# One encoder trunk on one core: the loading stage and the first input stage put into one program per engine

## The reference

```python
hn = rms_norm(x, norm_mix[0])                      # y = x * rsqrt(mean(x*x) + 1e-6) * gain
proj = hn @ w_in                                   # 2560 columns: u (1024), q, k, v (512 each)
u = u[..., :512] * sigmoid(u[..., 512:])           # the gating ("glu")
u = silu(layer_norm(depthwise_conv(u, width=31) + conv_b, ln_g, ln_b))
lam = exp(sum(lq1 * lk1)) - exp(sum(lq2 * lk2)) + 0.2
a = softmax(q0 k0 + bias) - lam * softmax(q1 k1 + bias)   # 4 heads, T5 bias from a 32-bucket table
h = h + concat(u, rms_norm(a @ v)) @ w_out         # then cross-attention on 256 tokens `mem`, then MLP
# layer 1: RWKV-7, forward and backward scans over 512 tokens, 16 heads of 64
w_pre = w0 + tanh(xw @ w1) @ w2                    # low-rank ("lora") pair for the decay
a_pre = a0 + (xa @ a1) @ a2                        # and for the in-context learning rate
```

## Time and profile before

| | |
|---|---|
| median of 3 runs | 2039.53 us |
| profiled execution, its own time | 2042.42 us |
| its span | 2040.6 us |
| PE busy | 1913.6 us (94%) |
| DVE busy | 1033.9 us (51%) |
| ACT busy | 740.0 us (36%) |
| POOL busy | 174.9 us (9%) |
| mean granted TensorE clock | 0.973 of full |

### The profile page before, as it was taken

How to read it: one execution, slowest core, us unless ns; L and a number is a source line. 1 busy time by engine, 2 the same in 40 slices (tenths; PEclk the granted TensorE clock), 3 DMA queues, 4 the chain that set the end, 5 groups by cost and what they waited for, 6 DMA issues and landing times. The chain is left out here.

```text
span 2040.6 us, 38376 instructions
## 1 busy us (share of the span) xinstructions
PE 1913.6 (94%) x16921; PEld 1544.4 (76%) x16921; DVE 1033.9 (51%) x1382; ACT 740.0 (36%) x991; POOL 174.9 (9%) x136
## 2 busy tenths in 40 slices
PE   6899799999999999899979999999689999999998
PEld 4788557778888888657758888889558778888886
DVE  4794365434433432464528877787254344424422
ACT  4331475325321332133733333332263334213322
POOL 1000002001000001220002311111001010000000
PEclk8999899999999999999989999999899999999998
DMA  5223414203332332244231111110443122332321
GB/s 181 83 83 124 144 55 158 92 22 102 103 104 87 99 104 85 101 147 149 78 129 42 47 47 47 48 47 25 144 175 104 42 83 83 103 103 83 104 83 41
DMA packets 162974, 187.82 MB, mean 92 GB/s; under 512 B 9657, under 2 KB 150118, under 8 KB 161402
## 3 DMA queue, kind: packets, MB, share of 16 engines
q1 hardware_dynamic: 159008, 172.48, 25.9%
q0 software_dynamic: 3152, 12.71, 1.6%
q10 hardware_dynamic: 650, 0.19, 0.0%
HBM read 160.18 MB, written 20.99 MB: 89 GB/s over the span
## 5 line engine op out<-in xcount | busy, mean ns | idle before, releaser
L332 DVE TENSOR_TENSOR weights_lo<-w,weights_hi 128x2048 fp32r<-128x2048 f32 x108 | 247.3, 2290 | 225.3 <-ACT weights_hi L319 225.3
L319 ACT ACTIVATE weights_hi<-w 128x2048 fp32r<-128x2048 f32 x110 | 210.2, 1911 | 259.9 <-PE ps L347 250.0
L345 PE MATMUL ps<-x_hn_hi,weights_hi 128*128 128x512 f32 x640 | 252.8, 395 | 0.0
L347 PE MATMUL ps<-x_hn_hi,weights_lo 128*128 128x512 f32 x640 | 249.2, 389 | 0.0
L346 PE MATMUL ps<-x_hn_lo,weights_hi 128*128 128x512 f32 x640 | 249.1, 389 | 0.0
L346 PE MATMUL ps<-f_hidden_lo,weights_hi 128*128 128x512 f32 x512 | 199.2, 389 | 0.0
L345 PE MATMUL ps<-f_hidden_hi,weights_hi 128*128 128x512 f32 x512 | 199.2, 389 | 0.0
L347 PE MATMUL ps<-f_hidden_hi,weights_lo 128*128 128x512 f32 x512 | 199.2, 389 | 0.0
L1461 DVE SCALAR_TENSOR_TENSOR f_relu<-ps,x_squares 128x512 f32<-128x512 f32 x64 | 44.1, 691 | 191.2 <-PE ps L347 172.6
L345 PEld LDWEIGHTS ps<-x_hn_hi,weights_hi 128*128 128x128 f32 x640 | 120.2, 188 | 26.3 <-issue 1.4
L346 PEld LDWEIGHTS ps<-x_hn_lo,weights_hi 128*128 128x128 f32 x640 | 120.2, 188 | 26.1 <-issue 1.4
(11 more groups left out here) (328 smaller groups left out, 3477.6 us busy)
## 6 DMA issues: line engine op xcount, KB each, us to landing
w<-in_ffn_w_up_dram SPq DMA_DIRECT2D x32, 1024.0 KB, 5.5
w<-in_ffn_w_down_dram SPq DMA_DIRECT2D x32, 1024.0 KB, 5.1
w<-in_xattn_w_kv_dram SPq DMA_DIRECT2D x16, 1024.0 KB, 5.4
w<-in_ab_w_in_dram SPq DMA_DIRECT2D x10, 1024.0 KB, 5.0
w<-in_xattn_w_q_dram SPq DMA_DIRECT2D x8, 1024.0 KB, 5.0
w<-in_xattn_w_o_dram SPq DMA_DIRECT2D x8, 1024.0 KB, 5.0
w<-in_ab_w_out_dram SPq DMA_DIRECT2D x4, 1024.0 KB, 5.4
w<-in_rwkv_w_r_dram SPq DMA_DIRECT2D x4, 1024.0 KB, 6.8
```

Source lines behind the costliest of these rows:

```text
L319: act.activation(hi, raw, ACT.Copy).then_inc(k.w_hi_ready, 1)
L332: eng.tensor_tensor(lo, raw, hi.bitcast(F32), ALU.subtract).then_inc(k.w_lo_ready, 1)
L345: pe.matmul(out, lhs[0], rhs[0], start=start, stop=False)
L347: return pe.matmul(out, lhs[1], rhs[0], start=False, stop=stop)
```

## The change

Four things are done in one diff.

1. The two blocks become one. The norm's root comes from sums over the rows of `x`: ACT squares the untransposed rows with an accumulating sum (L680), takes Ln and Exp of the 128x4 result, DVE scales four identity matrices by it (`x_roots`), and PE multiplies ones by these, which leaves the root of every token on all partitions in PSUM bank 7; the norm reads it there. PE transposes the parameter rows first, then `x`. DVE takes five of the eight transposed chunks out of the banks, ACT three. The bias table rows ("b") and lambda's sums ("l") move into `seq` behind i2. The small loads move from ACT's queue to SP's, and SP loads one weight slot ahead of them and two behind.
2. `glu(1)` stands after 24 steps of the convolution.
3. POOL no longer waits for the memory values at the stage's end. ACT (before the first write over the region) and POOL (at its own end) wait for them in the next stage. SP issues the bias reload ahead of the last three weight slots.
4. In the scan the lora tiles of pair p + 2 are issued behind the later of W and A of pair p.

```diff
 class Norm:                       # start_dve
-        dve.wait_ge(self.s_rs, 1)
...
-                                         self.rs[:, 1, :], ALU.mult, ALU.mult).then_inc(self.s_t, 1)
+                                         k.ps[:, 7, :], ALU.mult, ALU.mult).then_inc(self.s_t, 1)
 def stage_in(k, cat):
         for n in range(16):
             seq.append(("i", n))
+            if n == 2:
+                seq += [("b", 0), ("b", 1), ("l", 0)]
...
             def _(sp):
-                sp.dma_start(k.con[:, :], i["consts"]).then_inc(s_con, 16)
+                sp.dma_start(k.con[:, 0:3 * P], i["consts"][:, 0:3 * P]).then_inc(s_con, 16)
...
+                sp.wait_ge(s_root, 1)
+                k.wait_full(sp, jx + C - 1)
+                sp.dma_start(mn, i["mem"][0].rearrange("(a p) d -> p a d", p=P)).then_inc(s_m, 16)
+                k.load_weights(sp, k.at)
+
+                sp.wait_ge(s_tvo, 16)
+                sp.wait_ge(s_ktout, 16)
+                sp.dma_start(k.bias[:, :, :], ...).then_inc(k.s_bias, 16)
+                k.load_weights(sp, k.at + NW)
...
             def _(pe):
+                pe.wait_ge(s_diag, 4)
+                for a in range(4):
+                    m = pe.matmul(k.ps[:, 7, a * P:(a + 1) * P], k.ones, diag[:, a, :], start=True, stop=True)
+                m.then_inc(s_rs, 1)
                 mm3_first(pe, k, j0, ws, hn, lambda c: nrm.wait(pe, c))
...
             def _(act):
+                act.wait_ge(s_eps, 1)
+                warm_ln(k, act)
+                for a in range(4):
+                    act.wait_ge(s_x[a], 16)
+                    k.act.link(act, act.activation(xsq[:, :], xn[:, a, :], ACT.Square, accum_out=xst[:, a:a + 1]))
+                k.act.link(act, act.activation(xst[:, 4:8], xst[:, 0:4], ACT.Ln, bias=k.eps[:, 0:1], scale=1.0 / D))
+                act.activation(xst[:, 8:12], xst[:, 4:8], ACT.Exp, scale=-0.5).then_inc(s_root, 1)
+                for c in (4, 6, 7):
+                    k.wait_full(act, jx + c)
+                    act.activation(k.h[:, c, :], k.bank(jx + c), ACT.Copy).then_inc(k.free(jx + c), 1)
                 nrm.start_act(act, ws)
...
             def _(dve):
                 ws.rest(dve, 2)
+                for b in range(2):
+                    jt = num["b", b]
+                    k.wait_full(dve, jt)
+                    dve.tensor_copy(tv[:, b * T:(b + 1) * T], k.bank(jt)[0:4, :]).then_inc(k.free(jt), 1)
                 glu(0)
                 ws.rest(dve, 3)
...
-                        if g == 0 and t == 18:
+                        if g == 0 and t == 12:
                             glu(1)
...
             def _(pool):
-                pool.wait_ge(s_vvout, 32)
...
 def stage_wkv(k):                 # SP's program; load_lora(p) is the lora part of the former load(p)
                 for kind, p in order:
-                    if kind == "vt":
+                    if kind == last_of(("W", "A"), p) and p + 2 < C:
+                        load_lora(p + 2)
+                    elif kind == "vt":
```

More of the change, by code:

```diff
@@ L565, in _ @@
[L565 to L586, removed]
@@ L590, in _ @@
                 pe.wait_ge(s_con, 16)
[L591 to L620, removed]
@@ new lines, in _ @@
+                pe.wait_ge(s_rows, 16 * len(ROWS[0]))
+                pe.wait_ge(s_rows2, 16 * (len(ROWS[1]) + len(ROWS[2])))
+                for g in range(3):
+                    n = sum(r for _, r in ROWS[g])
+                    k.take(pe, jp + g)
+                    pe.transpose(k.bank(jp + g)[:, 0:n], rows[0:n, g, :], k.ident[0:n, 0:n]).then_inc(k.done(jp + g), 1)
+                for c in range(C):
+                    k.take(pe, jx + c)
+                    for a in range(4):
+                        pe.wait_ge(s_x[a], 16)
+                        m = pe.transpose(k.bank(jx + c)[:, a * P:(a + 1) * P], xn[:, a, c * P:(c + 1) * P], k.ident)
+                    m.then_inc(k.done(jx + c), 1)
@@ L702, in _ @@
                         m = mm3_chunks(pe, k, num[x], ws, n // 2, (n % 2) * P, hn)
+                    elif kind == "b":
+                        k.take(pe, num[x])
+                        pe.wait_ge(s_small, 16 * 7)
+                        m = pe.matmul(k.bank(num[x])[0:4, :], tab[:, :], oneh[:, n * T:(n + 1) * T], start=True, stop=True)
+                    elif kind == "l":
+                        k.take(pe, num[x])
+                        pe.wait_ge(s_lq, 1)
+                        m = pe.matmul(k.bank(num[x])[:, 0:2], k.ones[0:64, :], lq[:, 4:6], start=True, stop=True)
                     elif kind == "m":
@@ L750, in _ @@
                         k.act.link(act, act.activation(mss[:, 4:6], mss[:, 2:4], ACT.Exp, scale=-0.5))
+                        jl = num["l", 0]
+                        k.wait_full(act, jl)
+                        k.act.link(act, act.activation(k.lam[:, 0:2], k.bank(jl)[:, 0:2], ACT.Exp))
+                        act.activation(k.lam[:, 2:3], k.lam[:, 0:1], ACT.Copy).then_inc(k.free(jl), 1)
                         for a in range(2):
@@ L864, in _ @@
             def _(pool):
+                load_rows(pool, 1, s_rows2)
+                load_rows(pool, 2, s_rows2)
                 pool.memset(up[:, :, :], 0.0).then_inc(s_pads, 1)
+                for b in range(2):
+                    k.wait_freed(pool, num["b", b])
+                pool.dma_start(k.tv_dram, tv[:, :]).then_inc(s_tvo, 16)
                 for n in range(8):
@@ L1975, in _, with load_lora @@
             def _(sp):
-                def load(p):
+                def load_lora(p):
                     if p >= 2:
                         full(sp, last_of(("W", "A"), p - 2), p - 2)
-                        full(sp, "VT", p - 2)
                     for a, src in enumerate((k.i["rwkv_w2"], k.i["rwkv_a2"])):
@@ L1983, in load @@
                               .then_inc(s_lora[p % 2], 16)
+                def load(p):
+                    if p >= 2:
+                        full(sp, "VT", p - 2)
                     if p == 0:
```

209 lines of the change are left out of this document (102 added, 107 removed).

## The result

| | before | after |
|---|---|---|
| median, run side by side on one chip | 2040.69 us (4 runs, 2036.05 to 2042.04) | 2012.87 us (4 runs, 2012.23 to 2017.34) |
| ratio after to before, 95% interval | | 0.9872 [0.9851, 0.9894] |
| profiled execution, its span | 2040.6 us | 2010.5 us |
| mean granted TensorE clock | 0.973 | 0.979 |

The change makes the kernel 27.8 us faster by the medians, 30.1 us by the spans of the two profiled executions, and about 26 us (22 to 30) by the ratio. The forecast was 36.2, to 2003.3, with a range of 1994 to 2013. The ratio on the 2039.53 that the forecast started from gives 2013.4, so the direction was right and the size too large, by 6 to 10 us according to the measure, which puts it at the outer edge of the range. First, where PE stands in the changed kernel.

A forecast was written before the change was run, and what follows sets the result against it. PE, busy 94% of the span, was taken as the bound, so its waits counted. Terms -11.0 + 0.5 + 3.2 - 7.2 - 1.9 - 7.0 - 1.0 - 11.8 = -36.2 took 2039.53 to 2003.3 us, range 1994 to 2013.

The forecast's parts named there:

- The beginning: Kernel start: PE's first large product at 23.3 instead of 34.37, minus 11.0 us (7.5 to 13).
- the insertion: Bias rows and lambda's sums behind i2: a new PE wait ahead of i3, plus 3.2 us (2.1 to 5).
- the second gating: Convolution: gating moved earlier removes PE's wait ahead of i9, minus 7.2 us, and its low clock, minus 1.9.
- the 0.5 for the first pair of jobs: After the first product: second slot's lo part holds up chunk 4, plus 0.5 us (0 to 2).
- the stage's end: Input stage's end: without POOL's wait the engines go on at 222.5 instead of 229.58, minus 7.0 us.
- The clock: Attention's start: PE's idle shrinks to 2.2 us, so its clock may stay high, minus 1.0 us (0 to 2).
- The scan: Lora tiles issued sooner: five of six PE waits go, some clock returns, minus 11.8 us (8 to 13).
- rival B: Scan: other waits replace those removed; if half the gain stays, 2009 us; chance 0.10.
- A: Beginning gives less, rows late or engines chained without overlap: first product at 28, 2008 us; chance 0.12.
- C: More than forecast: wait at i3 goes to nothing and the scan runs more evenly, 1997 us; chance 0.08.
- D: Second gating: DVE too early or late again; if the wait returns whole with its clock, 2012 us; chance 0.06.
- E: Slower: PE's clock stays at 1.2 GHz after the first product, i0 to i9; ten such jobs, 2051 us; chance 0.04.

The follow-up runs named there:

- experiment 7: Kernel before with only the second gating moved from the 18th to the 12th pair of convolution steps: 2031.55 us, ratio 0.9954.
- experiment 3: Changed kernel with POOL's explicit wait for the memory values put back at the input stage's end: 2016.66 us, ratio 0.9874.
- experiment 6: Kernel before with only POOL's wait for the memory values moved into the next stage: 2039.56 us, ratio 0.9996.
- experiment 1: Changed kernel with POOL issuing the last memory values first in the attention stage instead of last in the input stage: 2007.72 us, ratio 0.9831.
- experiment 5: Changed kernel with SP instead of POOL issuing the last memory values at the input stage's end: 2004.31 us, ratio 0.9818.
- experiment 2: Changed kernel with SP's last of three weight slots loaded ahead left to the attention stage: 2011.71 us, ratio 0.9851.
- experiment 11: Kernel before with POOL's wait moved a stage later, SP issuing the last memory values, and the bias reload ahead of SP's last three slots: 2032.40 us, ratio 0.9964.
- experiment 9: Kernel before with POOL's wait moved into the next stage and SP issuing the last memory values: 2036.16 us, ratio 0.9970.
- experiment 8: Kernel before with only the scan's lora tiles issued sooner: 2032.61 us, ratio 0.9960.
- experiment 10: Changed kernel with SP issuing the last memory values, i2's gating before the bias-row copies, and the first weight slot's rounding and lo part earlier: 2002.98 us, ratio 0.9807.

## Why the prediction was right or wrong

Differences between the two profiled executions at seven places and over the whole span, beside the terms (positive is time gained):

| place | before | after | gained there | forecast |
|---|---|---|---|---|
| first large product | 34.37 | 23.15 | 11.2 | 11.0 |
| i1 done (ACT's sigmoid) | 47.25 | 35.95 | +0.1 | -0.5 |
| gating of i3 | 58.88 | 51.05 | -3.5 | -3.2 |
| i9 done (ACT takes q) | 101.12 | 84.11 | 9.2 | 7.2 + 1.9 |
| attention's first product | 229.58 | 210.75 | 1.8 | 7.0 |
| first W of the scan | 1053.67 | 1033.50 | 1.3 | 1.0 |
| last W of the scan | 1354.17 | 1323.64 | 10.4 | 11.8 |
| span | 2040.6 | 2010.5 | -0.4 | 0 |

**The beginning, the insertion and the second gating** came out as worked, each within 0.6 us, and experiment 7 confirms the third by itself. The sum at i9 was 17.0 against 16.4 forecast. Only the 0.5 for the first pair of jobs had the wrong sign.

**The step that failed is the stage's end.** "Without it the engines meet at 221.95 and go on after 0.58" took the written wait for what held the engines. It was redundant: with it or without it (experiments 3 and 6) PE stands equally long within 0.4 us. What holds the engines is that POOL itself has a DMA in flight: the wait goes when the same transfer is issued a stage later (1) or by SP (5), and it stays when SP's transfer is moved instead (2), only shortened by as much as POOL's lands sooner. The size of the term was right for a change that removes the cause: experiment 11 gains 7.5 in the old kernel (5 to 10 by the ratio's interval), against 8.0. What was gained here, 1.8, is the landing itself: POOL's values took 7.5 us in the kernel before, beside the bias reload, and 5.7 in the changed one, where the reload has gone out earlier. No run has the sooner reload alone, so that this is its doing is argued and not shown. The bound given in the prediction, "Least gain 5, if the reload or the last weights tie the stage to a DMA after all", named the wrong DMAs and was no lower bound: the real gain was 1.8. The forecast's own test, "the attention's start still tied to a DMA", is what came.

The clock hung on the same step. After 7.48 of idle PE ran at 0.50 until about 214, as it did behind the meeting before the change, so none of the 1.3 at the first W in the table is the clock's; after the 1.83 of experiments 1 and 5 its four products took 1.13 instead of 2.08.

The prediction read from two rows, 2.22 high and 2.71 low, that "the edge lies about there". The other traces show no such edge. Idles of 1.79, 1.83 and 1.83 ahead of the attention kept the high clock, and 2.42 (experiment 9) was followed by 0.62 in the window from 222 to 224. But in the scan of experiment 11 an idle of only 2.04 ahead of a W at 1248.29 was followed by 0.73 and then 0.50 (windows of 2 us), while the 2.22 of the earlier trace rows was followed by 1.00 for the next 6 us, and in experiment 7 the eight products behind an idle of 2.83 still took 1.11, and the clock fell only behind them. The Trainium skill, "TensorE: Matmul & The Clock Gate", Part 1, says that the point of change varies with its phase. These traces agree with that: an idle of 2 to 3 us cost nothing in one place and the clock in another.

**The scan** was over-sized too. The mechanism was right: five waits gone, the first stays, in the full change and alone, and the periods shrink from 48.0 to 46.0 us (mean of five, between the first W products of the third and the last pair), as said. But over all the traces the sum of the waits did not come back in full. From the first W product to the end of the last the eight profiled kernels with the sooner lora tiles take 290.8 to 296.7 us, mean 294.0 (the changed kernel is the fastest of them); the five without take 300.4 to 303.2, mean 301.7. So it is worth 7.7 rather than 11.8, and experiment 8's median says 7.1. The pair before and after alone would have said 10, since the changed kernel's scan is the shortest of the eight. The two ends are in the rows of the W products (start of the first, end of the last), before, after and in experiment 1:

```profile
L2055 PE MATMUL ps<-w_hidden,s_lora_outer x64: 589/640/1112, 1053.7 to 1354.7; 64*64 64x512 f32 x64
```

```profile
L2050 PE MATMUL ps<-w_hidden,s_lora_outer x64: 589/589/1109, 1033.5 to 1324.3; 64*64 64x512 f32 x64
```

```profile
L2050 PE MATMUL ps<-w_hidden,s_lora_outer x64: 589/589/1113, 1023.3 to 1320.0; 64*64 64x512 f32 x64
```

In the five kernels without it the five waits sum to 10.3 to 12.3 us, mean 11.3, so about a third does not come back, and what takes it isn't settled. In experiment 8 idles of PE grew at places that the profile puts down to no one, here in that kernel's scan and then in the scan of before:

```profile
PE ps L2170 <- issue: 4.5, 2, 2.7
...
PE ps L2095 <- issue: 2.9, 1, 2.9
```

```profile
PE ps L2163 <- issue: 2.7, 3, 1.3
```

Some of these may be records that are missing, so they don't prove rival B. As to B itself, half the gain going to new waits: about a third of the waits' sum went, to something.

**What else moves.** From the attention's first product to the first W the thirteen profiled executions take 818.2 to 824.1 us, though the programs are alike there but for one DMA at the head. The four that enter with the high clock and the bias in place (experiments 1, 5, 10, 11) have a mean of 820.0, the eight that enter with the low clock 822.1; that difference is of the size of the clock's term, but the two groups overlap. So the last W of two kernels can differ by 3 us for no reason of the change, and the medians (27.8) and the spans (30.1) of before and after need not agree better. Putting the two over-sized terms right (the stage's end with its clock 1.8 instead of 8.0, the scan 7.7 instead of 11.8), 36.2 - 6.2 - 4.1 = 25.9, stands beside 27.8 by the medians, 30.1 by the spans and 26 by the ratio.

**The rivals.** A, C, D and E did not come: the first product was on time, the wait at i3 was there, the gating was in time, and PE's clock rose after the first products (from 26.56 on each took 0.39 us instead of 0.63). B came at most in part. The largest miss lay at a place for which no rival was written.

## What to carry to other kernels

Before a wait is priced as removable, ask what else would hold the engines at that very moment; here a stage's end was held by POOL's own DMA, whether a wait for it was written or not. In this kernel the last transfers of a stage belong on SP's queue, or at the head of the next stage: with that, PE's idle at the meeting was 1.8 us instead of 7.5. And a wait that is removed may have the next late thing close behind it: in experiment 9 PE went on 7.8 us sooner and DVE's first score came only 2.4 sooner, because the bias reload was late. Look for that thing and move both.

## What the runs showed of the hardware

- A DMA issued by POOL holds the meeting of the engines until it has landed (PE idle 7.48 and 7.81 us, going on 0.8 and 1.4 after the landing), one issued by SP does not (1.83 us, with 1 MB and 256 KB of SP's in flight). Why isn't shown by these runs: whether the chip does it, or something that is put at a block's end when the program is built, stays open, and a DMA issued by ACT was not tried.
- POOL's 256 KB took 5.7 us to land beside a 1 MB load issued 0.9 us earlier, and 2.5 us without it (experiment 2).
- In the changed kernel the Ln and the Exp of the root have a table load of 1.28 us between them; the root over 128x4 elements costs 0.30 + 1.28 + 0.20 of ACT, and most of that is the load. Before, the same load stood between L421 and L422.
- An idle of 2 to 3 us had no fixed effect on PE's clock: behind 2.22 us it stayed at 1.00, behind 2.04 us (experiment 11) it was 0.73 and then 0.50.
